# Constant products at TensorE's waits in the chunked mixers of a hybrid recurrent decoder step

## The reference, cut to what matters

```python
def step(S, inp):
    qi, ki, vi, Gi = inp
    ...
    o = einsum('bhij,bhjv->bhiv', s, vi) + einsum('bhid,bhdv->bhiv', qi * exp(Gi), S)
    S = S * exp(g_end)[:, :, 0, :, None] + einsum('bhjd,bhjv->bhdv', ki * exp(g_end - Gi), vi)
```

## Time and profile before

| | us |
|---|---|
| median of 3 runs | 2664.91 |
| lowest, highest | 2664.61, 2672.33 |
| span of the profiled execution | 2669.7 |
| PE busy | 2361.5 (88%) |
| DVE, ACT, POOL busy | 1143.3, 707.0, 878.4 |
| mean granted TensorE clock over the span | 0.934 |

### The profile page before, as it was taken

How to read it: one execution, slowest core, us unless ns; L and a number is a source line. 1 busy time by engine, 2 the same in 40 slices (tenths; PEclk the granted TensorE clock), 3 DMA queues, 4 the chain that set the end, 5 groups by cost and what they waited for, 6 DMA issues and landing times. The chain is left out here.

```text
span 2669.7 us, 46576 instructions
## 1 busy us (share of the span) xinstructions
PE 2361.5 (88%) x20608; PEld 2174.2 (81%) x20608; DVE 1143.3 (43%) x1558; ACT 707.0 (26%) x891; POOL 878.4 (33%) x620
## 2 busy tenths in 40 slices
PE   5988887788899999999988889777898999999997
PEld 3867876678778989999978779656787798999997
DVE  5175465465444532221233556645735356222212
ACT  2432311411213232222224332114112223222222
POOL 2322310133233434444432123102423244444442
PEclk8989987889999989999989899878999999999998
DMA  6331121111222333322233311211112322222222
GB/s 253 117 114 65 56 69 64 41 44 45 83 95 96 116 100 119 119 92 87 92 117 116 112 56 59 81 52 33 52 53 76 124 76 96 88 95 88 88 95 72
DMA packets 68457, 233.38 MB, mean 87 GB/s; under 512 B 10785, under 2 KB 11297, under 8 KB 67873
## 3 DMA queue, kind: packets, MB, share of 16 engines
q1 hardware_dynamic: 61344, 214.88, 24.1%
q10 hardware_dynamic: 6912, 15.53, 1.6%
HBM read 219.03 MB, written 11.35 MB: 86 GB/s over the span
## 5 line engine op out<-in xcount | busy, mean ns | idle before, releaser
L740 POOL TENSOR_TENSOR ring_lo<-ring,w_hi 128x512 fp32r<-128x512 f32 x552 | 767.7, 1412 | 1334.5 <-ACT w_hi L1365 1308.9
L808 PE MATMUL gm<-H_hi,ring_lo 128*128 128x260 f32 x3456 | 745.0, 297 | 64.5 <-DVE H_lo L1775 21.5
L808 PE MATMUL gm<-H_hi,w_hi 128*128 128x260 f32 x3456 | 715.3, 288 | 0.1
L808 PE MATMUL gm<-H_lo,w_hi 128*128 128x260 f32 x3456 | 714.3, 289 | 0.3 <-issue 0.3
L808 PEld LDWEIGHTS gm<-H_hi,ring_lo 128*128 128x128 f32 x3456 | 555.6, 195 | 104.8 <-issue 23.7
L808 PEld LDWEIGHTS gm<-H_hi,w_hi 128*128 128x128 f32 x3456 | 548.4, 194 | 1.9 <-issue 1.1
L808 PEld LDWEIGHTS gm<-H_lo,w_hi 128*128 128x128 f32 x3456 | 548.8, 194 | 0.9 <-issue 0.5
L1365 ACT ACTIVATE w_hi<-ring 128x1024 fp32r<-128x1024 f32 x250 | 264.0, 1056 | 449.6 <-PE gm L808 186.1
L757 POOL TENSOR_TENSOR X<-X,GT 128x520 f32<-128x520 f32 x32 | 48.8, 1526 | 303.6 <-DVE GT L2295 303.6
L1289 PE MATMUL gm<-AF_hi,ring_lo 128*128 128x260 f32 x704 | 142.1, 283 | 3.3 <-DVE AF_lo L2319 3.3
L1289 PE MATMUL gm<-AF_hi,w_hi 128*128 128x260 f32 x704 | 141.6, 282 | 0.0
(11 more groups left out here) (408 smaller groups left out, 2799.9 us busy)
## 6 DMA issues: line engine op xcount, KB each, us to landing
ring<-wall SPq DMA_DIRECT2D x372, 512.0 KB, 3.4
WB<-wbranch SPq DMA_DIRECT2D x32, 256.0 KB, 3.7
xsave<-X SPq DMA_DIRECT2D x2, 2080.0 KB, 12.0
X<-xsave ACTq DMA_DIRECT2D x8, 520.0 KB, 5.2
arena<-states ACTq DMA_DIRECT2D x8, 512.0 KB, 3.3
sst<-arena ACTq DMA_DIRECT2D x8, 512.0 KB, 3.6
X<-xt SPq DMA_DIRECT2D x1, 2080.0 KB, 12.2
y<-H SPq DMA_DIRECT2D x4, 520.0 KB, 2.7
```

Of the source, the lines that this page charges most:

```text
L740: pool.tensor_tensor(ring_lo[:, SLOT[i], k], ring[:, SLOT[i], k], hi[:, k].bitcast(F32), ALU.subtract).then_inc(parts_ready, 1)
L808: ins = pe.matmul(out[:, hf, 0:HALF], w[a][:, k, :], src[b][:, k, HALF * hf:HALF * (hf + 1)], start=first and a == "lo", stop=last and a == b)
```

## The change

`operands` gets a parameter `bank`. With it, `keep_busy` writes to columns 256 to 383 of that bank of `mx`, whether or not a `gm` bank is open. Three of the four waits of `inverse` get 5 products each when the mixer is RW. The waits of `chunk` get 3 products each for HG (one wait per chunk) and 4 for RW (three waits per chunk); GD and RT get none. The first wait of `inverse` stays as it is, and so does the last one of the odd chunks.

```diff
+BUSY_INVERSE, BUSY_CHUNK = 5, {HG: 3, RW: 4, GD: 0, RT: 0}
...
-                def operands(most=FILL, sem=operands_v, busy=0):
+                def operands(most=FILL, sem=operands_v, busy=0, bank=None):
                     fill(most)
-                    keep_busy(busy)
+                    keep_busy(busy, None if bank is None else mx[:, bank, 256:256 + P128])
                     pe.wait_ge(sem, count.next(sem))
...
-                def inverse(cp):
-
+                def inverse(n, cp):
+
+                    busy = BUSY_INVERSE if n == RW else 0
...
-                    operands(FILL_SHORT, operands_a)
+                    operands(FILL_SHORT, operands_a, busy, 3)
...
-                    operands(FILL_SHORT)
+                    operands(FILL_SHORT, busy=busy, bank=3)
...
-                    operands(FILL_SHORT, operands_a)
+                    operands(FILL_SHORT, operands_a, busy, 0)
...
-                    operands(FILL_CHUNK)
+                    busy = BUSY_CHUNK[n]
+                    operands(FILL_CHUNK, busy=busy, bank=1)
...
-                        operands(FILL_CHUNK)
+                        operands(FILL_CHUNK, busy=busy, bank=3)
...
-                        operands(FILL_CHUNK)
+                        operands(FILL_CHUNK, busy=busy, bank=3)
```

More of the change, by code:

```diff
@@ L1157, in rwkv @@
                         yield
-                        yield from inverse(cp)
+                        yield from inverse(RW, cp)
                         for ci in range(2):
@@ L1219, in gdn @@
                         yield
-                        yield from inverse(cp)
+                        yield from inverse(GD, cp)
                         for ci in range(2):
```

## The result

The changed kernel takes 2685.73 us (median of 4 runs, 2677.5 to 2690.89), the kernel before beside it 2664.76 us (2659.91 to 2672.33). The ratio is 1.0068 with a 95% interval of 1.0044 to 1.0092: 21 us slower, against a forecast of 19. A second set of 5 runs gave 2684.23 us against 2666.83, ratio 1.0051 (1.0019 to 1.0083).

The account below looks back on a forecast made before the run. PE's ordered queue, busy 88% of the span, was taken as the bound. RW's 13.6 + 23.1 - 13 = 24 us and HG's -5 gave +19 us on 2664.9, so 2684 us, range 2655 to 2702 us.

Parts of the forecast that it names:

- RW's inverses, first group to last: Constants in RW's four inverses stick out of the idle times at half clock, 13.6 us slower in all.
- the rest of RW's stages, clock gain taken off: RW's chunks: constants cost 23.1 us, less 13 us won back by a sooner full clock.
- Price of a constant: On PE, one constant product costs 0.22 us at full clock and 0.43 us at half clock.
- Filled waits of RW's chunks: RW's chunks 0, 1 and 3: no idle time, so 0.88 us paid at each of nine waits, 7.9 us a layer.
- Inverses at half clock: RW's inverses: five constants take 2.15 us against idle 0.88, 1.43 and 0.74 us; 3.4 us stick out in a pair.
- No rise in the inverses: RW's inverses: small products between the constants keep the clock low, with no rise before the first chunk.
- the forecast case: Whole kernel: RW 24 us slower, HG 5 us faster, 19 us slower in sum; 2675 to 2695 us, chance 0.50.
- rival 1: The clock rises in RW's inverses too, after the first five constants; each gains about 1 us; 2656 us, chance 0.17.
- What the clock gives back: RW's chunks: removing all half-clock time is worth 17 us; three quarters taken, 13 us.
- HG, -5 us: HG's chunks: a sooner full clock saves about 14 us against 8.6 us of constants, net 5 us faster.
- Rival 3, absorption: PE's 20.5 us waits for POOL's rest of the weights shrink and absorb the delay; 2665 us, chance 0.08.
- Rival 4: No clock gain anywhere, so the constants cost their full 45 us; 2710 us, chance 0.10.

Follow-up runs that it names:

- the fastest kernel: Kernel holding the clock up ahead of RW's inverses, plus 6, 2, 2 constants in RW's chunk 2 and 3 in HG's chunk 0: 2637.73 us, 0.9881 of the kernel before.

## Why the prediction was right

The mechanism came as forecast in RW's stages. That the total did too (+21 for +19) owes something to luck. Between the first two profiles, 19.4 us apart:

| us | forecast | measured |
|---|---|---|
| RW's inverses, first group to last (L1009 to L1027) | +13.6 | +13.7 |
| the rest of RW's stages, clock gain taken off | +10.1 | +7.3 |
| HG's stage | -5 | -6.7 |
| everything else | 0 | +5.1 |

- **Price of a constant:** 0.22 us forecast at full clock, 0.22 measured by doubling the constants in the chunks.
- **Filled waits of RW's chunks:** paid in full, as forecast, 0.89 us for four. Chunk 1 is longer by 1.77 us and not by 2.6, since only two of its three waits lie inside these marks; the third shows as 0.88 us more ahead of its first product.
- **Inverses at half clock:** 3.4 us forecast for each, 4.0 measured in the first pairs and 4.4 in the second. The term was too small because five constants hold the product behind them for 2.43 us (382.74 to 385.17) and not for 5 x 0.43 = 2.15: that product, of another tile size, starts only when the last constant has nearly ended (385.24). I had priced the distance between like products; behind four constants in a chunk, a product of the full tile size starts after 0.89 us = 4 x 0.22. The sum of 13.7 came out right only because the one inverse in which the clock rose cost 1.2 us.
- **No rise in the inverses:** right for three of four, in both profiles of the changed kernel and in the run with the inverses alone. So the forecast case came with one inverse in four as in rival 1.
- **Rival 1**, which decided the sign, was put after the first five constants, and in one inverse of four the clock rose just there. But its price was wrong: the inverse was 1.16 us longer (7.94 against 6.78) and not 1 us shorter. Shorter are only the inverses that are at full clock from their start on, in the two runs that held the clock up ahead of them (8.5 us against 10.3 to 10.9).
- **What the clock gives back:** 13 us forecast for RW's chunks. By the table they won back about 16 in the full change. With the chunks alone RW's stages were 12.4 us longer, so about 11 of the 23.1 us came back. The rest came mostly behind the one inverse in which the clock rose: chunk 2 there takes 9.33 us, where it is 12.57 with the chunks alone.
- **HG, -5 us:** -6.7 in this pair of traces, +0.2 against the second profile of the kernel before, no more than about 4 us of gain on average, and not to be seen in the time of HG alone. The term was wrong in that I read the cost of the low clock from one execution, in which that stage happened to be near its slowest (18.2 and 19.7 us of 13.1 to 19.7). The total came out right in part because another 5 us outside these stages took its place.
- **Rival 3, absorption:** did not happen; PE's wait for POOL's `ring_lo`, 20.5 us before, was 19.3 after. **Rival 4:** not reached, since the chunks did win clock time.

PE was at half clock through 14.93 busy us of 14.95 in layer 1's second inverse, and at full clock through HG's chunks with 14.34 of 14.87. The Trainium skill says that activity releases the throttle ("TensorE: Matmul & The Clock Gate", Part 1). The rows of HG's chunks agree; in the inverse the engine was busy throughout, and the throttle was not released in those 14.95 us.

## What to carry to other kernels

Work put in only to hold TensorE's clock is free where it stands as far as it fits into idle time that the trace shows at that very wait, and is paid in full everywhere else; count it wait by wait, at the clock that the stretch has, and put none where real work already fills the wait. Put it at the wait at which the clock falls, and not only at those that follow: 126 products, from there on and counted to the idle times, were worth 29 us, 180 behind it cost 21. (No run has those at the first wait alone.) Time the whole kernel as well, for what is hidden where it stands can still cost elsewhere, as below. And read a stage that depends on the clock from several profiles before its slow time is booked as something to win.

## What was not expected

A change that costs nothing where it stands can cost 8 us elsewhere. Twelve hidden products in layer 0's and layer 1's idle wait made the kernel 8 us slower, the same twelve in layer 1 alone nothing. The waits of PE that the views put down to nothing ('issue'), nearly all in front of HG's 32-column score products, were, in the full change (its first profile), the idle-wait run, the one in layer 1 alone and the fastest kernel:

```profile
PE mx L980 <- issue: 9.2, 5, 4.0
...
PE mx L980 <- issue: 9.7, 6, 3.5
...
PE mx L980 <- issue: 6.9, 5, 2.6
...
PE mx L980 <- issue: 5.8, 4, 2.1
```

**What these waits are.** The DMA records of the traces show it. The DMA queue of kind "instruction" (`q8`) brings blocks of 16 KiB, 162 of them before and 165 with the 720 more instructions of the changed kernel (weight loads counted in), so it brings PE's code:

```profile
q8 instruction: 165, 2.70, 0.4%
```

In the thirteen profiles there are 79 such waits, and in every one PE goes on 1.20 to 1.60 us after one of these blocks has landed, though blocks come 3 to 9 us apart there. The longest, 6.7 us in the second profile of the full change, ended at 1506.93 us, 1.34 us after a block that was on its way from 1504.64 to 1505.59 us:

```profile
PE mx L980 <- issue: 11.2, 5, 6.7
```

So PE waits there for its own code, where it runs through many short products. Why one block is asked for later than another isn't shown.

**What they explain.** In layer 0, ahead of which nothing was added, they sum to 1.7 to 4.1 us in all thirteen profiles. In layer 1, ahead of HG's stage, they sum to 1.5 and 4.6 us in the two profiles of the kernel before and 4.1 in the run with layer 1's constants alone, to 6.1 to 8.8 in the nine profiles with something added ahead, and to 3.0 in the fastest kernel, which has as much added ahead. The full change had 9.4 us in all in its first profile, where the kernel before had 3.3: that is 6.1 us, enough for the 5.1 outside the stages. That added code makes these waits longer is likely but not shown: the fastest kernel speaks against it. They don't explain the 8 us of the idle-wait run: against the run in layer 1 alone it has 2.8 us more of them, in two profiles that are 19.8 us apart, and 8.3 us more in HG's stage (18.2 and 19.7 us against 16.6 and 13.1), of which 1.6 lie in layer 0, ahead of any change. Nor does the low clock of HG's stage in layer 1 follow them: it took 19.7 us behind 1.5 to 8.1 us of such waits, and 13.05 us behind 4.1 to 8.4. Where those 8 us come from is open.
